# Two-block f32 forward pass on one core: expert panels in a ring of four groups of three, rows of 48 KB

## The chip, the core and the metric

One core of one Trainium2 chip runs the whole program. TensorE (PE) multiplies, VectorE (DVE) and ScalarE (ACT) work on what it leaves in PSUM, SyncE (SP) issues nearly all transfers from device memory (HBM) to the on-chip memory (SBUF, 128 partitions), and 16 DMA engines carry them. The metric is the device time of one execution in microseconds (us); the median of several executions stands for a kernel. The PE clock has two levels, 1.2 and 2.4 GHz; a granted clock of 1.00 in a stretch means the upper one throughout.

## The reference

Two blocks in sequence on 256 tokens of width 1024, all in f32. The first is a mixer (sliding-window attention, block attention, gated delta rule) and a gated feed-forward. The second puts 16 meta tokens in front (T = 272), runs a convolution branch and a bidirectional state-space branch, merges them, and ends with a mixture of experts. The end of the second block is what the change touches:

```python
branch_ssm  = y @ w_ssm_out                      # "ssm_out": 8 panels
branch_conf = ... @ w_conf_out                   # "conf_out": 4 panels
h = h + (gate_a * branch_conf + gate_b * branch_ssm) @ w_out     # "w_out_2": 4 panels
hn = rms_norm_2(h, w_norm_ffn)
aff = softmax(hn @ w_router)                     # 16 experts
top_aff, top_idx = top_k(aff.T, 34)              # each expert picks 34 of 272 tokens
for e in range(16):
    xg = hn[top_idx[e]]                          # 34 x 1024
    y[e] = (silu(xg @ w_gate[e]) * (xg @ w_up[e])) @ w_down[e]
h = h + scatter of top_aff[e] * y[e]
out = rms_norm_2(h[16:], w_norm_final)
```

Each expert has three matrices of 1024 x 2048 or 2048 x 1024 f32, 25.17 MB together; the 16 experts are 402.7 MB. Each weight is used once.

## The kernel before

All matrices are packed on the way in as panels, one contiguous row per partition. A panel of the dense stages is 128 x 2048 f32 (1.05 MB, rows of 8 KB). They go through two slots (`dense`, `slot_loaded`, `panel_done`, helper `panel` of SP's program, L370): SP issues the next panel into a slot when PE has finished the slot's last one. PE needs 32 matmuls, 7.37 us, for a panel of the second block.

An expert is twelve panels q = 0 to 11 of 128 x 4096 f32 (2.10 MB): q = 0 to 7 hold gate and up (even q is gate, odd q is up, one pair for each p = 0 to 3), q = 8 to 11 hold down. SBUF has a ring of `RING` = 12 slots, one for each q. The tensor `in_experts` is laid out as [16, 6, 128, 8192]: two neighbouring panels share a row of 32 KB. SP's program fills the ring with one transfer for two slots (`both[i]`, L474) where the slots are neighbours in SBUF, and slots 10 and 11 one by one (L477, L483). It waits until PE has released both (`ring_done[q]`). So an expert comes in five transfers of 4.19 MB with rows of 32 KB and two of 2.10 MB with rows of 16 KB.

Expert 0 is brought in during the stages before, slot by slot (`expert_panel`, L425; slot 11 at L403, near 120 us of the trace): each slot of the ring lies over buffers of an earlier stage and can be filled when they are dead. Slots 2 to 5 go behind the last four `ssm_out` panels, 10 behind the second `conf_out` panel, 0, 1 and 7 within and behind the `w_out_2` panels, then 6, 8 and 9. "Routing" is the short stage between the last `w_out_2` panel (near 873 us) and expert 0 (893.57 us): the logits, the softmax, the top-k and the first gather, with the turning of the tokens (`turn_tokens_of`) behind the logits.

Expert 1 replaces expert 0 in slots 0 to 3 by column parts, as soon as PE has read those columns (L461, `first_parts`). From slot 4 of expert 1 on, the loop at L462 to L486 runs. For the last expert, slots 6 and 7 come in two halves, 8 and 9 apart, 10 in two parts and 11 in three.

PE takes an expert in this order (`expert` for the first and last, `middle_expert` in a loop for the others): p = 0 reads slots 0 and 1 together; p = 1 reads slots 2 and 3, then the gather of the next expert's tokens; p = 2 reads 4 and 5; p = 3 reads 6 and 7; then slots 8 and 9, the scatter of the expert before, and slots 10 and 11. Every pair of slots is 32 matmul records of 128x512, some 7 us. PE waits on `pair_loaded[p]` ahead of each pair.

Of the kernel before, what the change touches and what calls it, by code (L numbers as in the profile page):

```python
# [11 lines left out]

# [10 lines left out]
P = 128  # L23
S = 256
META = 16
T = META + S
D = 1024
DC = D // P
PW = 256
# [9 lines left out]
E = 16  # L39
# [7 lines left out]
def pair_arrivals(i, e):  # L47

    return 2 + e + ((4 if i == 0 else 3) if i < 2 and e else 0)
# [29 lines left out]
def _run(kind, first, last):  # L79
# [29 lines left out]
             "last2_loaded": ("small_loaded", 16), "last9_loaded": ("last9_loaded", 0), "last10_loaded": ("last10_loaded", 0), "last_up": ("last_up", 0), "last3_loaded": ("rows_loaded", 16), "lgT_copied": ("wT_copied", 1), "lgT_done": ("res_ready", 4), "lg_done": ("heads_done", 2),  # L109
# [16 lines left out]
def two_blocks(nc, a, out):  # L126

    with ExitStack() as ctx:
# [174 lines left out]
        top[0] = upper  # L303
        cut(4 * 4096)
        es, up_row = cut(512), cut(512)
        lg, pos_t, aff = cut(3, E), cut(3, E), cut(3, E + 1)
        lmx, rst = cut(3), cut(3)
        m8 = cut(8)
        ss = cut(3, 4)
        xg = cut(DC, CAP)  # L310
        sum_col = cut(32)
        assert top[0] <= ARENA - 4096
# [6 lines left out]
        top[0] = mark1 - 512 - 2 * DC * T + 4096  # L319
        otT = [cut(S) for _ in range(2)]  # L320
        assert top[0] <= mark1
        top[0] = mark1 + 8192
        h_tok = cut(2, D)
        xt = cut(2 * 512)
        ysb, last_y = xt[64:64 + CAP, :], xt[0:CAP, 0:512]
        ones_r = cut(T)
        ohg, ohs = cut(2, CAP), cut(2, CAP)
        assert top[0] <= upper - 8192
        top[0] = mark1 - 512 - 2 * DC * T + 4096
        left, pos = cut(T), cut(T)  # L330
        assert top[0] <= mark1
        top[0] = low + 8192
        h_row = cut(2, 512)
        hx = cut(EB, CAP)
        assert top[0] <= base_dense + 2 * 11 * PW + DC * T
        pair_loaded = [ev(f"pair{i}_loaded") for i in range(5)]
        slot10_loaded, slot11_loaded = ev("slot10_loaded"), ev("slot11_loaded")
# [28 lines left out]
        def _(sp):  # L366
# [36 lines left out]
            sp.dma_start(ring[11], a["experts"][0, 5][:, 4096:8192]).then_inc(slot11_loaded, 16)  # L403
# [18 lines left out]
            def expert_panel(e, q):  # L422

                arrived = slot10_loaded if q == 10 else pair_loaded[q // 2]
                sp.dma_start(ring[q], a["experts"][e, q // 2][:, q % 2 * 4096:q % 2 * 4096 + 4096]).then_inc(arrived, 16)  # L425
# [12 lines left out]
            for g in range(4):  # L438
                panel(PANELS["w_out_2"] + g)
                if g == 1:  # L440
                    sp.wait_ge(ev("merged_ready"), after["merged_ready"] + 4)
                    expert_panel(0, 0)
            expert_panel(0, 1)
            expert_panel(0, 7)
            for last in (n[0] - 2, n[0] - 1):
                sp.wait_ge(panel_done[last % 2], last // 2 + 1)
            expert_panel(0, 6)
            sp.wait_ge(ev("lgT_done"), after["lgT_done"] + 1)
            expert_panel(0, 8)
            sp.wait_ge(ev("hacc_turned"), after["hacc_turned"] + 2)  # L450
            expert_panel(0, 9)
            in_parts = lambda ap: ap.rearrange("p (x m) -> p x m", x=2)
            for i, edges in enumerate(((0, 512, 1024, 2048, 3072, 4096), (0, 1024, 2048, 3072, 4096))):
                for j, (lo, hi) in enumerate(zip(edges, edges[1:])):
                    if hi < 4096:
                        sp.wait_ge(ev("first_parts"), after["first_parts"] + 4 * i + j + 1)
                    else:
                        sp.wait_ge(ring_done[2 * i], 1)
                        sp.wait_ge(ring_done[2 * i + 1], 1)
                    part = slice(lo, hi)  # L460
                    sp.dma_start(in_parts(both[i])[:, :, part], in_parts(a["experts"][1, i])[:, :, part]).then_inc(pair_loaded[i], 16)  # L461
            for e in range(1, E):  # L462
                for i in range(2 if e == 1 else 0, 5):
                    sp.wait_ge(ring_done[2 * i], e)
                    sp.wait_ge(ring_done[2 * i + 1], e)
                    if i == 4 and e + 1 == E:
                        sp.dma_start(ring[8], a["experts"][e, 4][:, 0:4096]).then_inc(pair_loaded[4], 16)
                        sp.dma_start(ring[9], a["experts"][e, 4][:, 4096:8192]).then_inc(ev("last9_loaded"), 16)
                    elif i == 3 and e + 1 == E:
                        for j, arrived in enumerate((pair_loaded[3], ev("last_up"))):  # L470
                            part = slice(2048 * j, 2048 * j + 2048)
                            sp.dma_start(in_parts(both[3])[:, :, part], in_parts(a["experts"][e, 3])[:, :, part]).then_inc(arrived, 16)
                    else:
                        sp.dma_start(both[i], a["experts"][e, i]).then_inc(pair_loaded[i], 16)  # L474
                sp.wait_ge(ring_done[10], e)
                if e + 1 < E:
                    sp.dma_start(ring[10], a["experts"][e, 5][:, 0:4096]).then_inc(slot10_loaded, 16)  # L477
                else:
                    for lo, arrived in ((0, slot10_loaded), (2048, ev("last10_loaded"))):
                        sp.dma_start(ring[10][:, lo:lo + 2048], a["experts"][e, 5][:, lo:lo + 2048]).then_inc(arrived, 16)  # L480
                sp.wait_ge(ring_done[11], e)
                if e + 1 < E:
                    sp.dma_start(ring[11], a["experts"][e, 5][:, 4096:8192]).then_inc(slot11_loaded, 16)  # L483
                else:
                    for lo, hi, arrived in ((0, 2, slot11_loaded), (2, 3, ev("last2_loaded")), (3, 4, ev("last3_loaded"))):
                        sp.dma_start(ring[11][:, 1024 * lo:1024 * hi],  # L486
                                     a["experts"][e, 5][:, 4096 + 1024 * lo:4096 + 1024 * hi]).then_inc(arrived, 16)
# [89 lines left out]
        def _(pe):  # L577
# [557 lines left out]
            pe.wait_ge(pair_loaded[1], 32)  # L1135
            for _ in range(6):
                mm(psum[:, 1, :], ident, ring[2][:, 0:512], start=True, stop=True)
# [1437 lines left out]
```

## Time and profile before

| | us |
|---|---|
| median of 3 runs | 1791.39 |
| lowest, highest | 1789.21, 1795.11 |
| the profiled execution, its own time | 1790.56 |
| its span in the trace | 1788.9 |
| start of the first expert's first matmul | 893.57 |
| start of the last expert's last 16 matmuls (slot 11) | 1775.52 |

The profile page gives busy time by engine (PE 1707.4 us, 95% of the span) and slices of the span. A busy share in a slice is an average. For the second half of this span two rows of the page have to be read side by side, that of PE and that of the DMA engines. PE counts as busy while its matmuls overlap, so a full PE row doesn't say that PE is what the end waits for; the waits do.

### The profile page before, as it was taken

The page shows a single profiled execution, that of the slowest core. Times are in us where ns is not written, and L with a number is a line of the kernel's source. Part 1 is how long each engine was busy: PE and PEld are TensorE (multiplying, and loading weights), DVE is VectorE, ACT ScalarE, POOL GpSimd, SP SyncE. Part 2 cuts the span into 40 slices and gives each one's busy share as a digit, 9 for nine tenths or more (in the row PEclk, how much of TensorE's full clock was granted, in tenths as well). Part 3 has the DMA queues.
Part 4 walks back from the last instruction along what each step waited for, and adds up shares of the span by engine and source line. Part 5 has one row for each costly group of instructions (what it writes and reads, how often), then busy time and mean ns, then how long its engine had stood idle before and what let it go on. Part 6 is the DMA issues. An engine that isn't in the chain of part 4 may idle for free.

```text
span 1788.9 us, 20978 instructions
## 1 busy us (share of the span) xinstructions
PE 1707.4 (95%) x8492; PEld 979.0 (55%) x8492; DVE 644.5 (36%) x1293; ACT 408.8 (23%) x783; POOL 32.3 (2%) x58
## 2 busy tenths in 40 slices
PE   9999999999999999999999999998988889998998
PEld 8778888887888888888723222322222222222222
DVE  3574466612759999941311101111010101111001
ACT  1143122201363544530111111111111111111112
POOL 4000000000000000100000000000000000000000
PEclk9999999999999999999999999989999999999989
DMA  5340244443453434376799999999999999999998
GB/s 187 118 189 13 83 158 148 163 148 115 167 191 118 167 129 169 108 284 250 311 388 432 430 428 435 428 432 432 431 430 431 430 430 434 430 432 428 435 431 332
DMA packets 36390, 523.08 MB, mean 292 GB/s; under 512 B 3880, under 2 KB 4072, under 8 KB 7784
## 3 DMA queue, kind: packets, MB, share of 16 engines
q1 hardware_dynamic: 35104, 511.75, 69.6%
q10 hardware_dynamic: 1224, 10.50, 1.6%
q8 instruction: 40, 0.66, 0.2%
q14 instruction: 22, 0.18, 0.0%
HBM read 521.12 MB, written 1.12 MB: 292 GB/s over the span
## 4 chain that ended last, share of the span: by engine, by line
PE 68%; DMA 27%; DVE 2%; SPq 1%; ACT 1%; issue 1%; DVEq 0%; another core or an unknown queue 0%; ACTq 0%
DMA arena<-in_experts 27%; PE psum L946 17%; PE psum L1301 12%; PE psum L597 12%; PE psum L1196 4%; PE psum L919 4%; PE psum L1030 3%; PE psum L1250 2%; PE psum L1011 1%; PE psum L660 1%; PE psum L681 1%; PE psum L899 1%; PE psum L1333 1%; PE psum L1220 1%; DMA arena<-in_panels 1%; SPq L480 1%
## 5 line engine op out<-in xcount | busy, mean ns | idle before, releaser
L1301 PE MATMUL psum<-arena 128*34 128x512 f32 x1792 | 412.2, 613 | 42.6 <-DMA arena<-in_experts 42.5
L2479 DVE SCALAR_TENSOR_TENSOR arena<-arena,psum 34x512 f32<-34x512 f32 x64 | 44.0, 687 | 759.5 <-ACT arena L1763 759.5
L946 PE MATMUL psum<-arena 128*128 128x272 f32 x1312 | 305.6, 392 | 0.0
L1301 PEld LDWEIGHTS psum<-arena 128*34 128x34 f32 x1792 | 106.5, 114 | 323.6 <-issue 279.1
L946 PEld LDWEIGHTS psum<-arena 128*128 128x128 f32 x1312 | 247.5, 189 | 53.2 <-issue 0.7
L1196 PE MATMUL psum<-arena 128*34 128x512 f32 x896 | 215.8, 637 | 9.8 <-DMA arena<-in_experts 9.8
L597 PE MATMUL psum<-arena 128*128 128x256 f32 x992 | 215.4, 378 | 0.0
L597 PEld LDWEIGHTS psum<-arena 128*128 128x128 f32 x992 | 187.2, 189 | 27.6 <-issue 1.2
L1196 PEld LDWEIGHTS psum<-arena 128*34 128x34 f32 x896 | 57.4, 118 | 157.9 <-issue 157.7
L1763 ACT ACTIVATE arena<-psum 34x512 f32<-34x512 f32 x64 | 37.9, 593 | 442.7 <-PE psum L1301 389.7
L2178 DVE SCALAR_TENSOR_TENSOR arena<-arena 128x272 f32<-128x272 f32 x240 | 111.0, 524 | 3.7
L919 PE MATMUL psum<-arena 128*128 128x256 f32 x352 | 76.4, 378 | 0.0
L919 PEld LDWEIGHTS psum<-arena 128*128 128x128 f32 x352 | 66.5, 189 | 9.7
L2166 DVE SCALAR_TENSOR_TENSOR arena<-arena 128x272 f32<-128x272 f32 x144 | 62.1, 498 | 6.6 <-ACT arena L1573 4.0
L1030 PE MATMUL psum<-arena 128*128 128x272 f32 x256 | 59.8, 392 | 0.1
L1250 PE MATMUL psum<-arena 128*34 128x512 f32 x256 | 56.4, 593 | 0.5 <-DVE arena L2460 0.5
L1783 ACT ACTIVATE arena<-psum 34x512 f32<-34x512 f32 x30 | 17.8, 592 | 169.1 <-PE psum L1196 161.8
L1333 PE MATMUL psum<-arena 34*128 34x512 f32 x112 | 55.0, 632 | 0.0
L1030 PEld LDWEIGHTS psum<-arena 128*128 128x128 f32 x256 | 48.3, 189 | 11.0 <-DMA arena<-in_panels 0.5
L2482 DVE SCALAR_TENSOR_TENSOR arena<-arena 34x512 f32<-34x512 f32 x64 | 44.0, 687 | 4.8
L1558 ACT ACTIVATE arena<-psum 128x544 f32<-128x544 f32 x34 | 21.2, 623 | 105.1 <-PE psum L946 103.8
L2098 DVE SCALAR_TENSOR_TENSOR arena<-arena 128x256 f32<-128x256 f32 x88 | 36.8, 482 | 4.5 <-issue 4.5
(449 smaller groups left out, 1368.9 us busy)
## 6 DMA issues: line engine op xcount, KB each, us to landing
arena<-in_experts SPq DMA_DIRECT2D x71, 4096.0 KB, 50.5
arena<-in_panels SPq DMA_DIRECT2D x91, 1024.0 KB, 4.8
arena<-in_experts SPq DMA_DIRECT2D x44, 2048.0 KB, 44.9
arena<-in_down_panels SPq DMA_DIRECT2D x8, 1408.0 KB, 6.0
arena<-in_experts SPq DMA_DIRECT2D x10, 1024.0 KB, 11.1
arena<-scr ACTq DMA_DIRECT2D x4, 2176.0 KB, 8.9
arena<-in_experts SPq DMA_DIRECT2D x4, 512.0 KB, 17.2
out<-arena SPq DMA_DIRECT2D x4, 256.0 KB, 2.1
```

Source lines behind the costliest of these rows:

```text
L597: ins = mm(pair[k][:, b, 0:width], slot8[k][:, c, b * P:(b + 1) * P], rhs(c), start=c == 0, stop=c == DC - 1)
L919: ins = mm(down_at(i)[:, b, :], slot11[k][:, c, b * P:(b + 1) * P], hid[:, 11 * j + c, :], start=j == 0 and i < 2 and c == 0, stop=j == 1 ...
L946: ins = mm(pair[k][:, b, 0:T], slot8[k][:, c, b * P:(b + 1) * P], src[:, c, :], start=c == 0, stop=c == DC - 1)
L1030: ins = mm(into[:, b, 0:T], slot8[k][:, c, b * P:(b + 1) * P], zT[:, 8 * j + c, :], start=j == 0 and c == 0, stop=j == 1 and c == DC - 1)
L1196: ins = mm(psum[64 * half:64 * half + CAP, 2, :], hx[:, f, :], r_dn[q][:, c, half * 512:(half + 1) * 512], start=f == 0, stop=f == EB - 1)
L1250: ins = mm(psum[lo:lo + CAP, p % 2, :], xg[:, c, :], r_up[2 * p + x][:, c, :], start=c == 0, stop=c == DC - 1)
L1301: ins = mm(psum[lo:lo + CAP, p % 2, :], xg[:, c, :], r_up[2 * p + x][:, c, :], start=c == 0, stop=c == DC - 1)
L1333: mm(psum[:, 4 + 2 * tb + half, :], otT[1 - par][64:64 + CAP, tb * P:(tb + 1) * P], ysb[:, half * 512:(half + 1) * 512], start=False, stop ...
L2166: ins = STT(gq[g % 2][:, b, :], xraw[g % 2][:, b, tap:tap + T], pcol("ssm_w", blk + 24 * tap), gq[g % 2][:, b, :], MUL, ADD)
L2178: STT(cc[:, c, :], cpad[:, c, tap:tap + T], pcol("conf_w", tap * DC + c), cc[:, c, :], MUL, ADD)
L2479: STT(es[gate_at, :], es[gate_at, :], 1.0, psum[gate_at, p % 2, :], ADD, MUL)
L2482: STT(h_row[turned_at, p % 2, :], es[gate_at, :], 0.5, up_row[gate_at, :], MUL, MUL).then_inc(ev("h_ready"), 1)
```

## The change

`in_experts` is laid out as [16, 4, 128, 12288]: three neighbouring panels share a row of 48 KB. The ring still has 12 slots, now in four groups of three (0 to 2, 3 to 5, 6 to 8, 9 to 11). Each group is contiguous in SBUF. The small buffers that lay between the slots move behind them. One transfer of 6.29 MB fills a group when PE has released all three of its slots. The exceptions are written out:

- Expert 0 still comes slot by slot. Slots 8, 7, 6 and 5 go behind the last four `ssm_out` panels, 4 behind the first `conf_out` panel, 3 behind the second, 2 where 0 was, then 1, 0, 9, and 10 with 11 in one. Nothing is loaded near 120 us.
- Expert 1: slots 0 and 1 in the same five parts; 2 and 3 in four parts, each part now two transfers; 4 and 5 in one.
- Expert 14 (last but one): its group 9 to 11 comes as 9 alone, then 10 with 11.
- Expert 15: 0 with 1, 2, 3, 4 with 5; from 6 on as before.

PE's arithmetic and its order are the same. Its waits ahead of the pairs become waits on groups: p = 0 on group 0, p = 1 and p = 2 on group 1, p = 3 and slot 8 on group 2, slot 9 on group 3. Three experts (13 to 15) are written out instead of one, and the loop runs six times instead of seven.

```diff
-        slots = [upper + 4096 * k for k in range(-2, 4)] + [mark1, mark1 + 4096, low, low + 4096, mark1 - 512 - 2 * DC * T, ARENA - 4096]
+        slots = [mark1 + 4096 * k for k in range(9)] + [low + 4096 * k for k in range(3)]
         ring = [arena[:, at:at + 4096] for at in slots]
-        both = [arena[:, slots[2 * i]:slots[2 * i] + 8192] for i in range(5)]
+        three = [arena[:, slots[3 * g]:slots[3 * g] + 3 * 4096] for g in range(4)]
...
-            sp.dma_start(ring[11], a["experts"][0, 5][:, 4096:8192]).then_inc(slot11_loaded, 16)
...
                 if i >= 4:
-                    expert_panel(0, i - 2)
+                    expert_panel(0, 12 - i)
             for g in range(4):
                 panel(PANELS["conf_out"] + g)
+                if g == 0:
+                    expert_panel(0, 4)
                 if g == 1:
-                    sp.wait_ge(ev("gates_tanh"), after["gates_tanh"] + 2)
-                    expert_panel(0, 10)
+                    sp.wait_ge(ev("conf_ready"), after["conf_ready"] + 1)
+                    expert_panel(0, 3)
...
-            expert_panel(0, 9)
+            sp.dma_start(three[3][:, 4096:], a["experts"][0, 3][:, 4096:]).then_inc(group_loaded[3], 16)
...
             for e in range(1, E):
-                for i in range(2 if e == 1 else 0, 5):
-                    sp.wait_ge(ring_done[2 * i], e)
-                    sp.wait_ge(ring_done[2 * i + 1], e)
...
+                for g in range(2 if e == 1 else 0, 4 if e + 2 < E else 3):
+                    for q in range(3 * g, 3 * g + 3):
+                        sp.wait_ge(ring_done[q], e)
+                    sp.dma_start(three[g], a["experts"][e, g]).then_inc(group_loaded[g], 16)
+            sp.wait_ge(ring_done[9], E - 2)
+            expert_panel(E - 2, 9)
+            for q in (10, 11):
+                sp.wait_ge(ring_done[q], E - 2)
+            sp.dma_start(three[3][:, 4096:], a["experts"][E - 2, 3][:, 4096:]).then_inc(ev("late_loaded"), 16)
...
                 for p in range(4):
-                    pe.wait_ge(pair_loaded[p], i * 32 + 16 * pair_arrivals(p, s + 1))
+                    pe.wait_ge(group_loaded[(0, 1, 1, 2)[p]], i * 32 + 16 * arrivals((0, 1, 1, 2)[p], s + 1))
```

The order of SP's transfers at three places. `in_panels` 128x2048 is a dense panel; `in_experts` 128x4096, 128x8192 and 128x12288 are one, two and three slots of the ring; the name behind "waits" is the semaphore (an event may share its semaphore's name with an older one: `bd_ready` is conf_ready, `o_copied` is gates_tanh).

SP from the last `ssm_out` panel's companion on, before:

```order
L425 DMA arena<-in_experts 128x4096
L370 DMA arena<-in_panels 128x2048 [waits panel_done1]
L370 DMA arena<-in_panels 128x2048 [waits panel_done0]
L425 DMA arena<-in_experts 128x4096 [waits o_copied]
L370 DMA arena<-in_panels 128x2048 [waits panel_done1]
```

and now:

```order
L426 DMA arena<-in_experts 128x4096
L372 DMA arena<-in_panels 128x2048 [waits panel_done1]
L426 DMA arena<-in_experts 128x4096
L372 DMA arena<-in_panels 128x2048 [waits panel_done0]
L426 DMA arena<-in_experts 128x4096 [waits bd_ready]
L372 DMA arena<-in_panels 128x2048 [waits panel_done1]
```

A slot of the ring (slot 4) now stands between the first and the second `conf_out` panel.

SP at the passage from expert 1's parts to the ring, from slots 4 and 5 of expert 1 on, before:

```order
L474 DMA arena<-in_experts 128x8192 [waits ring5_done,ring4_done]
L474 DMA arena<-in_experts 128x8192 [waits ring7_done,ring6_done]
L474 DMA arena<-in_experts 128x8192 [waits ring9_done,ring8_done]
L477 DMA arena<-in_experts 128x4096 [waits ring10_done]
L483 DMA arena<-in_experts 128x4096 [waits ring11_done]
L474 DMA arena<-in_experts 128x8192 [waits ring1_done,ring0_done]
```

and now:

```order
L475 DMA arena<-in_experts 128x8192 [waits ring5_done,ring4_done]
L482 DMA arena<-in_experts 128x12288 [waits ring8_done,ring7_done,ring6_done]
L482 DMA arena<-in_experts 128x12288 [waits ring11_done,ring10_done,ring9_done]
L482 DMA arena<-in_experts 128x12288 [waits ring2_done,ring1_done,ring0_done]
L482 DMA arena<-in_experts 128x12288 [waits ring5_done,ring4_done,ring3_done]
```

The transfer behind slots 4 and 5 now waits for slot 8 as well as for 6 and 7.

SP at the end, from expert 14's slots 6 and 7 on, before (the first two rows end expert 14's pairs):

```order
L474 DMA arena<-in_experts 128x8192 [waits ring7_done,ring6_done]
L474 DMA arena<-in_experts 128x8192 [waits ring9_done,ring8_done]
L477 DMA arena<-in_experts 128x4096 [waits ring10_done]
L483 DMA arena<-in_experts 128x4096 [waits ring11_done]
L474 DMA arena<-in_experts 128x8192 [waits ring1_done,ring0_done]
L474 DMA arena<-in_experts 128x8192 [waits ring3_done,ring2_done]
L474 DMA arena<-in_experts 128x8192 [waits ring5_done,ring4_done]
L472 DMA arena<-in_experts 128x2x2048 [waits ring7_done,ring6_done]
```

and now:

```order
L482 DMA arena<-in_experts 128x12288 [waits ring5_done,ring4_done,ring3_done]
L482 DMA arena<-in_experts 128x12288 [waits ring8_done,ring7_done,ring6_done]
L426 DMA arena<-in_experts 128x4096 [waits ring9_done]
L487 DMA arena<-in_experts 128x8192 [waits ring11_done,ring10_done]
L490 DMA arena<-in_experts 128x8192 [waits ring1_done,ring0_done]
L426 DMA arena<-in_experts 128x4096 [waits ring2_done]
L426 DMA arena<-in_experts 128x4096 [waits ring3_done]
L496 DMA arena<-in_experts 128x8192 [waits ring5_done,ring4_done]
L501 DMA arena<-in_experts 128x2x2048 [waits ring7_done,ring6_done]
```

Expert 14's slots 3 to 8 arrive in two transfers of three where they came in pairs and singles; what follows them is of the old sizes.

## Rows read from the trace of the kernel before

**Rows 1.** The page: span, and busy share of the DMA engines in 40 slices

```profile
span 1788.9 us, 20978 instructions
DMA  5340244443453434376799999999999999999998
```

**Rows 2.** Windows: us; busy us of each engine; PE clock, DMA share, GB/s

```profile
777.00:812.00 35.00, 34.91 (x152) 28.43 (x151) 8.73 (x5) 13.20 (x14) 0.00 (x0) 1.00 0.97 384
890.00:895.00 5.00, 4.46 (x31) 2.34 (x29) 1.97 (x6) 0.59 (x1) 0.00 (x0) 1.00 0.04 16
905.00:915.00 10.00, 10.00 (x48) 2.69 (x46) 1.38 (x2) 2.37 (x4) 0.00 (x0) 1.00 1.02 408
895.00:927.80 32.80, 32.80 (x166) 9.64 (x164) 6.75 (x13) 6.71 (x12) 0.00 (x0) 1.00 0.99 382
1174.00:1641.00 467.00, 424.08 (x1904) 130.16 (x1904) 54.17 (x104) 66.29 (x120) 0.00 (x0) 0.95 1.00 431
1755.00:1775.00 20.00, 19.80 (x103) 6.01 (x98) 2.75 (x4) 4.45 (x7) 0.00 (x0) 1.00 1.01 422
```

**Rows 3.** Timeline of PE, 1425 to 1500 us: start, duration, instructions, [idle before]

```profile
1437.22 7.08 PE L1301 MATMUL psum<-arena 128*34 128x512 f32 x32 [1.24 <-DMA arena<-in_experts]
...
1446.76 8.77 PE L1301 MATMUL psum<-arena 128*34 128x512 f32 x32 [2.06 <-DMA arena<-in_experts]
...
1495.58 4.92 PE L1301 MATMUL psum<-arena 128*34 128x512 f32 x22 [1.24 <-DMA arena<-in_experts]
```

**Rows 4.** DMA: SP's queue (packets, MB, share); issues by size, median to landing

```profile
q1 hardware_dynamic: 35104, 511.75, 69.6%
...
arena<-in_experts SPq DMA_DIRECT2D x71, 4096.0 KB, 50.5
...
arena<-in_experts SPq DMA_DIRECT2D x44, 2048.0 KB, 44.9
```

**Rows 5.** SP's timeline near 806 us, the chain there, and PE's timeline

```profile
806.42 8.05 SPq L370 DMA_DIRECT2D arena<-in_panels  x2
814.52 0.43 SPq L425 DMA_DIRECT2D arena<-in_experts  x1
...
799.06 7.38 DMA arena<-in_panels
...
813.95 29.63 PE L946 MATMUL psum<-arena 128*128 128x272 f32 x128
```

**Rows 6.** Timelines of SP and PE from routing into expert 1

```profile
858.70 23.94 SPq L425 DMA_DIRECT2D arena<-in_experts  x5
...
916.70 8.10 SPq L474 DMA_DIRECT2D arena<-in_experts  x2
...
925.06 7.06 PE L1220 MATMUL psum<-arena 128*34 128x512 f32 x32
...
947.68 7.08 PE L1301 MATMUL psum<-arena 128*34 128x512 f32 x32
```

**Rows 7.** PE: one undisturbed expert, then the end; SP's line L486 (slot 11)

```profile
1103.54 7.08 PE L1301 MATMUL psum<-arena 128*34 128x512 f32 x32
...
1145.87 4.47 PE L1301 MATMUL psum<-arena 128*34 128x512 f32 x20
...
1699.65 8.70 PE L1301 MATMUL psum<-arena 128*34 128x512 f32 x32 [1.80 <-DMA arena<-in_experts]
...
1721.37 9.76 PE L1196 MATMUL psum<-arena 128*34 128x512 f32 x32
1730.97 7.05 PE L1250 MATMUL psum<-arena 128*34 128x512 f32 x32
...
1775.52 3.63 PE L1220 MATMUL psum<-arena 128*34 128x512 f32 x16 [0.41 <-DMA arena<-in_experts]
...
L486 SPq DMA_DIRECT2D arena<-in_experts x3: 2135/2399/5725, 1740.4 to 1748.6; - x3
DMA to landing us min/median/max: 29.4/30.6/35.1
```

More of the change, by code:

```diff
@@ L44, with arrivals @@
 ARENA = 57048
-def pair_arrivals(i, e):
-    return 2 + e + ((4 if i == 0 else 3) if i < 2 and e else 0)
+def arrivals(g, e):
+    return (3, 3, 3, 2)[g] + e + ((4, 8, 0, 0)[g] if e else 0)
 SQ = {"x": 0, "qk": 4, "o": 5, "mix": 6, "h": 11, "ffn": 15, "h1": 20, "conf": 24}
@@ new lines, in two_blocks @@
+        h_tok = small(2, D)
+        xt = small(2 * 512)
+        ysb, last_y = xt[64:64 + CAP, :], xt[0:CAP, 0:512]
+        ones_r = small(T)
+        ohg, ohs = small(2, CAP), small(2, CAP)
+        es, up_row = small(512), small(512)
+        lg, pos_t, aff = small(3, E), small(3, E), small(3, E + 1)
+        lmx, rst = small(3), small(3)
+        m8 = small(8)
+        ss = small(3, 4)
+        xg = small(DC, CAP)
+        sum_col = small(32)
+        top[0] = low + 3 * 4096
+        left, pos = cut(T), cut(T)
@@ L320, in two_blocks @@
+        top[0] = low + 3 * 4096
+        h_row = cut(2, 512)
+        hx = cut(EB, CAP)
         otT = [cut(S) for _ in range(2)]
         assert top[0] <= mark1
[L322 to L337, printed above, removed]
+        group_loaded = [ev(f"group{g}_loaded") for g in range(4)]
         ring_done = [ev(f"ring{k}_done") for k in range(RING)]
@@ L450, in _ @@
             sp.wait_ge(ev("hacc_turned"), after["hacc_turned"] + 2)
-            expert_panel(0, 9)
[L452 to L461, printed above, removed]
@@ L462, in _ @@
-            for e in range(1, E):
-                for i in range(2 if e == 1 else 0, 5):
-                    sp.wait_ge(ring_done[2 * i], e)
-                    sp.wait_ge(ring_done[2 * i + 1], e)
[L466 to L487, printed above, removed]
@@ new lines, in _ @@
+            sp.dma_start(three[3][:, 4096:], a["experts"][0, 3][:, 4096:]).then_inc(group_loaded[3], 16)
+            pairs = lambda ap: ap.rearrange("p (x m) -> p x m", x=2)
+            edges = (0, 512, 1024, 2048, 3072, 4096)
+            for j, (lo, hi) in enumerate(zip(edges, edges[1:])):
+                if hi < 4096:
+                    sp.wait_ge(ev("first_parts"), after["first_parts"] + j + 1)
+                else:
+                    sp.wait_ge(ring_done[0], 1)
+                    sp.wait_ge(ring_done[1], 1)
+                sp.dma_start(pairs(three[0][:, 0:8192])[:, :, lo:hi],
+                             pairs(a["experts"][1, 0][:, 0:8192])[:, :, lo:hi]).then_inc(group_loaded[0], 16)
@@ new lines, in _ @@
+            for j in range(4):
+                if j < 3:
+                    sp.wait_ge(ev("first_parts"), after["first_parts"] + 5 + j)
+                else:
+                    sp.wait_ge(ring_done[2], 1)
+                    sp.wait_ge(ring_done[3], 1)
+                for q in (2, 3):
+                    expert_panel(1, q, group_loaded[1], 1024 * j, 1024 * j + 1024)
+            for q in (4, 5):
+                sp.wait_ge(ring_done[q], 1)
+            sp.dma_start(three[1][:, 4096:], a["experts"][1, 1][:, 4096:]).then_inc(group_loaded[1], 16)
@@ new lines, in _ @@
+            sp.dma_start(three[3][:, 4096:], a["experts"][E - 2, 3][:, 4096:]).then_inc(ev("late_loaded"), 16)
+            for q in (0, 1):
+                sp.wait_ge(ring_done[q], E - 1)
+            sp.dma_start(three[0][:, 0:8192], a["experts"][E - 1, 0][:, 0:8192]).then_inc(group_loaded[0], 16)
+            for q in (2, 3):
+                sp.wait_ge(ring_done[q], E - 1)
+                expert_panel(E - 1, q, ev("last1_loaded"))
+            for q in (4, 5):
+                sp.wait_ge(ring_done[q], E - 1)
@@ new lines, in _ @@
+            sp.dma_start(three[1][:, 4096:], a["experts"][E - 1, 1][:, 4096:]).then_inc(group_loaded[1], 16)
+            sp.wait_ge(ring_done[6], E - 1)
+            sp.wait_ge(ring_done[7], E - 1)
+            for j, arrived in enumerate((group_loaded[2], ev("last_up"))):
+                part = slice(2048 * j, 2048 * j + 2048)
+                sp.dma_start(pairs(three[2][:, 0:8192])[:, :, part],
+                             pairs(a["experts"][E - 1, 2][:, 0:8192])[:, :, part]).then_inc(arrived, 16)
@@ L1335, in middle_expert @@
                 pe.wait_ge(ev("hx_copied"), i * 4 + (2 * s + 4))
-                pe.wait_ge(slot10_loaded, i * 32 + 16 * (s + 2))
                 down_panel(10)
-                pe.wait_ge(slot11_loaded, i * 32 + 16 * (s + 2))
                 down_panel(11)
             expert(0)
-            with pe.Fori(0, (E - 2) // 2) as i:
+            with pe.Fori(0, (E - 4) // 2) as i:
                 for s in range(2):
                     middle_expert(i, s)
-            expert(E - 1)
+            for e in range(E - 3, E):
+                expert(e)
             scatter(E - 1)
```

73 lines of the change are left out of this document (41 added, 32 removed).

## The prediction

> **What bounds the kernel now.** I read the slices first. From about half the span on, the DMA engines are full to the end [rows 1]. That is the expert stage. The window from 1174 to 1641 us gives the load there: DMA share 1.00 at 431 GB/s, while PE is busy 424 of 467 us [rows 2]. PE's timeline says who waits: pairs of slots begin behind idle time that a transfer of in_experts ended, and the first pair of one expert begins 58.36 us after that of the one before (1437.22, 1495.58) [rows 3]. An expert is 25.17 MB, so 58.36 us is 431.2 GB/s. Undisturbed, PE needs less: one expert, from its second pair (1103.54) to the next one's first (1145.87) took 42.33 us [rows 7], and with the first pair and what goes with it about 51. So the end is set by a sum: when the DMA engines become full for good, the bytes left over their rate, and what PE still has to do once the last bytes are there. The change can move all three.
>
> **The larger rows.** Does the rate depend on the row? First, what counts as a packet. Each transfer of in_experts, in_panels and their like has 128 rows, or 256 where a part covers two slots (11 transfers). SP issues 234 transfers, 71 and 44 of them the large and the single ones of the ring [rows 4]. That makes 234 x 128 + 11 x 128 = 31,360 rows, and 16 completions for each transfer make 3,744 more: 35,104, which is the queue's count of packets exactly [rows 4]. So a row of 32 KB is one packet, and an engine handles 8 + 1 packets for a transfer of 128 rows. An expert costs it 7 x 9 = 63.
>
> The price of a packet comes from stretches that are full but cut finer. 1755 to 1775 us carries the last four slots in seven transfers: 63 packets where the ring has 21 for the same bytes, at 422 GB/s against 431 [rows 2]. 8.39 MB take 19.88 us against 19.45: 0.43 us for 42 packets, 10 ns each. 905 to 915 us carries parts with rows of 4 KB at 408 [rows 2]: 4.08 MB in 66 packets against 10, 0.54 us more, 9.6 ns. I take 10 ns.
>
> The change has 53 transfers of three slots, 333 MB or 13.25 experts. They cost 53 x 9 = 477 packets where the ring before has 13.25 x 63 = 835. The gain is 358 x 10 ns = **-3.6 us** (the ring at 433 GB/s). Its ends are 0, if a row of 48 KB is cut or something else holds the rate, and 13.6 ns a packet (what solving the ring and the last four slots with slightly other roundings gives), -4.9.
>
> The Trainium skill (DMA: Bandwidth & Descriptors, Bandwidth) puts the fabric's ceiling at 435.2 GB/s. By that, an expert's excess over the ceiling would be 0.54 us over 63 packets, 8.6 ns, and the gain -3.1 instead of -3.6.
>
> **The gap at group 2 of expert 1.** Before, the transfer of slots 6 and 7 is issued near 924.5, at the end of the two L474 issues that begin at 916.70 [rows 6]. From 895 to 927.8 the engines move 382 GB/s x 32.8 us = 12.5 MB [rows 2], which is slots 0 to 5 of expert 1 (12.58). So that transfer is there 3 us ahead of need. Now it also waits for slot 8. PE reads 8 and 9 in the 7.06 us from 925.06 [rows 6], so slot 8 is released at 928.6; the first bytes follow some 1.3 us behind the issue (an estimate, with ends of 0.3 and 2.0: at the panels below, bytes and what PE sees of them lie 1.8 us apart). The engines stand from 927.9 to about 930: **+2.1 us** (1.0 to 2.8). Every byte behind is moved by that, since the engines don't stand again: the next group is released near 940.3, while group 2 lasts to 944.5; group 0 of expert 2 is released when slots 2 and 3 are read, 954.6 (947.68 + 6.9) [rows 6], while group 3 lasts to 959; the lead then grows by 7 us with each expert.
>
> The idle time ahead of that, 890 to 895 at 16 GB/s [rows 2], is filled: slots 10 and 11 (4.19 MB in place of 2.10) are issued at the end of the five, 882.6 [rows 6], and last until 894. That costs nothing, since expert 1's first part is issued at 894.67 and PE needs slot 10 only near 933. It also gives nothing: the slot that moved there was free before, at 120 us. Slot 0, issued near 873 instead of 845, lands by 880 for a use at 893.57.
>
> **The conf_out panels.** From 777 to 812 us panels and slots share the engines at 384 GB/s [rows 2]. A panel is issued when its slot is released and is needed 7.37 us later. The one issued at 799.06 took 7.38, and the first conf_out panel (806.42) was begun at 813.95, 0.1 us late [rows 5]. By 806.42 four slots and five panels were issued, 13.6 MB, 13.4 of them in that window; so the engines were through at about 812.2, 1.8 us ahead of 813.95. Nothing is late again. Now slot 4 stands behind the panel of 806.42. It lasts to 812.2 + 5.2 = 817.4; the second panel (814.1) to 820.1, and seen 1.8 us behind, 821.9, for a need at 821.3. Slot 3 (in place of slot 10 at 814.52 [rows 5]) ends at 825.2, the third panel at 827.9, seen at 829.7 for a need at 829.3. **+0.9 us** on PE's path (0 if the engines move 431 there, 1.6 at the low end). PE's path leads through routing to the first parts, so the full stretch starts that much later.
>
> The wait of slot 3 for conf_ready costs nothing: PE waits for the same event before 813.95. PE's own waits on groups 0 to 3 for expert 0 are on slots landed 10 us or more ahead. The finer parts of slots 2 and 3 have the same rows as before. The unrolled experts have the same matmuls; I cost them at nothing.
>
> **The last two experts.** This is the term one overlooks. Before, PE ends level with the transfers: its last 16 matmuls begin at 1775.52 after 0.41 us of waiting and end at 1779.15; the last piece, issued at 1748.6, lands 29.4 later, at 1778.0 [rows 7]. Call that T. PE got there with no wait worth naming since 1699.65 [rows 7]. So anything that starts PE's last run later against T shows.
>
> Now the run starts earlier in the program but later against T. Expert 14's p = 1 waits for group 1. Behind its landing come group 2 (14.5 us), 9 to 11 (14.6) and expert 15 (58.8): it lands at T - 87.9. PE is idle some 6 us before it, since p = 0 needs group 0 alone, 14.5 us earlier. Such pairs mostly took 8.77 us where 7.08 is normal [rows 3], +1.7. Then 42.3 us to the next expert's first pair [rows 7], and from there to the end of slot 11 47.6 (1730.97 to 1779.15, less 0.6 of waits) [rows 7]; no piece lands later than PE wants it. Sum: T - 87.9 + 1.7 + 42.3 + 47.6 = T + 3.7, against T + 1.15 before: +2.5. A run of 91 us without a wait mostly holds one more slow stretch like 1721.37 (9.76 for 7.06) [rows 7]; I add 1.5 for it. **+4.0 us** (0.8 with neither, 5.8 with a long one).
>
> **Sum.** -3.6 + 2.1 + 0.9 + 4.0 = +3.4. The profiled execution took 1790.56, so 1794.0; it lies 0.83 below the median of 1791.39, so 1794.8 as a median.
>
> **Rivals.**
> A, the end is not late. If PE runs its last pairs at full clock and the gap at 928 is covered (the release comes while engines still work off expert 0's last slots), the terms are -3.6 + 1.0 + 0.5 + 0.8 = -1.3: 1790.1. For it: the bytes end and slot 8 is released within 1 us, and some pairs behind a wait ran at 7.08. Against: PE's wait before p = 1 is the longest of an expert. 0.18.
> B, the whole excess goes. The ring's 0.63 us per expert over 25.17 MB at 435.9 GB/s (the rate that 10 ns leaves) belongs to the pitch of 32 KB, not to packets, and 48 KB lifts all of it: 13.25 x 0.63 = -8.3, sum -1.3, 1790.1; with A's other terms, -6.0, 1785.4. For it: fine rows and the pitch can't be told apart in one trace. Against: the two finer stretches fit one price. 0.10. The Trainium skill (DMA: Bandwidth & Descriptors, Latency and other measured facts) has copies slowed by row pitches that are large powers of two, from 512 KB on; nothing here shows it at 32 KB.
> C, slower. Rows of 48 KB bring nothing: the ring keeps 431 GB/s, because a longer row is carried as two packets or a limit elsewhere holds. The losses stand: +7.0, 1798.4. The point from which this decides against the change is 3 ns a packet. For it: no row above 32 KB is in the trace. Against: 32 KB goes as one. 0.17.
> D, the panels are hit harder: if a longer run of both kinds loses twice what 777 to 812 us lost against the ring (337 GB/s), the two panels come 2.0 and 1.9 us late, +3.9 for 0.9, sum +6.4: 1797.8. 0.05.
> My forecast: 0.50.
>
> **Numbers.** A measurement of this kernel can tell about 0.3%, 5.4 us, from no change. The forecast's own spread, 1790.5 to 1798, is mostly inside; C and D are outside on the slow side, part of B on the fast. I add a little on the fast side for what isn't seen: faster 0.14, same 0.58, slower 0.28. The range runs from A and most of B to C and D with the medians' own 2 us: 1787 to 1800.
>
> **What would show it.** Right: the ring at 433 GB/s and an expert every 58.1 us; PE's share of windows alike; the engines standing near 929; in expert 15, PE with no wait on transfers and its last matmuls 3 to 6 us behind the last landing; SP's queue with fewer packets by exactly the count of rows and completions. Wrong: an expert still at 58.36 us (C), at 57.8 (B), last matmuls level with the last landing (A), conf_out panels begun more than 2 us late (D).

## The result and the profile after

| | before | changed | ratio, 95% interval |
|---|---|---|---|
| median, us (22 runs each) | 1791.24 | 1794.09 | 1.0018 [1.0011, 1.0024] |
| lowest, highest | 1788.32, 1795.11 | 1792.56, 1800.77 | |
| span in the trace | 1788.9 | 1791.8 | |

The changed kernel is 2.9 us slower, a small loss that 22 runs show clearly and that three would not. The forecast was 1794.8, 3.4 slower.

The page of the changed kernel, its span, its DMA slices, SP's queue, and the issues that answer to [rows 1, 4]:

```profile
span 1791.8 us, 20893 instructions
DMA  4330244433453444377799999999999999999997
...
q1 hardware_dynamic: 29408, 511.75, 69.4%
...
arena<-in_experts SPq DMA_DIRECT2D x53, 6144.0 KB, 40.5
```

The same bytes go in 29,408 packets where it was 35,104. The 5,696 that are gone are 356 for each of 16 engines. So a row of 48 KB is one packet too: an engine now handles 8 rows and one completion for three slots.

The windows that answer to [rows 2], and one more, of the end (us; busy time of each engine; PE clock, DMA share, GB/s), of the changed kernel:

```profile
777.00:812.00 35.00, 34.59 (x151) 28.15 (x150) 8.73 (x5) 12.36 (x13) 0.00 (x0) 1.00 0.99 396
...
890.00:895.00 5.00, 4.47 (x31) 2.39 (x29) 1.97 (x6) 0.59 (x1) 0.00 (x0) 1.00 0.99 421
...
925.00:935.00 10.00, 9.51 (x55) 3.32 (x56) 2.66 (x7) 1.41 (x3) 0.00 (x0) 1.00 0.94 374
1174.00:1641.00 467.00, 422.85 (x1917) 126.28 (x1915) 55.06 (x106) 67.67 (x122) 0.00 (x0) 0.94 1.00 433
```

```profile
1690.00:1745.00 55.00, 55.00 (x244) 16.69 (x241) 6.36 (x11) 8.69 (x16) 0.00 (x0) 0.95 0.99 426
```

Two windows of the kernel before that [rows 2] doesn't have:

```profile
925.00:935.00 10.00, 9.51 (x52) 3.03 (x52) 2.66 (x7) 1.01 (x3) 0.00 (x0) 1.00 0.99 424
1690.00:1745.00 55.00, 52.86 (x221) 16.16 (x223) 4.97 (x9) 6.56 (x13) 0.00 (x0) 0.91 1.01 432
```

The ring moves 433 GB/s, which was forecast; it was 431. The time before 895 us, empty in the kernel before, is full. In 925 to 935 us, where the kernel before has 424, the engines stand for a part: 374. In 1690 to 1745 us PE is busy without a pause; it was 52.86 of 55.00.

PE's timeline, which answers to [rows 3, 7]. First the second pair (p = 1) of two experts in the ring, then the last two experts, and the issue of the last two pieces:

```profile
1282.00 8.90 PE L1325 MATMUL psum<-arena 128*34 128x512 f32 x32 [6.49 <-DMA arena<-in_experts]
...
1340.06 8.77 PE L1325 MATMUL psum<-arena 128*34 128x512 f32 x32 [4.73 <-DMA arena<-in_experts]
```

```profile
1689.48 9.95 PE L1274 MATMUL psum<-arena 128*34 128x512 f32 x32 [5.30 <-DMA arena<-in_experts]
...
1771.51 10.50 PE L1241 MATMUL psum<-arena 128*34 128x512 f32 x48
...
L426 SPq DMA_DIRECT2D arena<-in_experts x2: 434/1262/2089, 1744.8 to 1747.0; - x2
DMA to landing us min/median/max: 31.3/31.7/32.1
```

PE now waits once per expert, for 4.7 to 6.7 us ahead of p = 1, where it mostly waited two to four times, for 1 to 2 us each. Two experts on, the same pair starts at 1398.26 and 1456.32; from 1165.72 to 1630.74 there are eight experts, 58.13 us each (it was 58.36). At the end there is no wait behind 1689.48: PE runs 92.5 us to 1782.01. The last piece is issued at 1747.0 and lands 31.3 later, at 1778.3; so PE ends 3.7 us behind it, where it was 1.15. The same distance was 3.7 to 5.3 us in all seven traces that leave the end as the change has it (the table in the section on why the prediction was right has them).

### The profile page after: what moved, and what is told of

It is laid out like the page before. It is cut to its first block, busy times and chain, and to the rows that moved or that the text cites. A ratio compares the mean times of both kernels' runs of the same rounds, so it can differ in the third digit from the quotient of the medians.

```text
span 1791.8 us, 20893 instructions
## 1 busy us (share of the span) xinstructions
PE 1701.8 (95%) x8490; PEld 971.4 (54%) x8490; DVE 644.8 (36%) x1293; ACT 409.9 (23%) x783; POOL 32.1 (2%) x58
## 3 DMA queue, kind: packets, MB, share of 16 engines
q1 hardware_dynamic: 29408, 511.75, 69.4%
## 4 chain that ended last, share of the span: by engine, by line
PE 70%; DMA 26%; DVE 2%; ACT 1%; issue 0%; DVEq 0%; ACTq 0%; SPq 0%
DMA arena<-in_experts 25%; PE psum L968 17%; PE psum L1325 12%; PE psum L619 12%; PE psum L1274 5%; PE psum L941 4%; PE psum L1052 3%; PE psum L1241 2%; PE psum L1218 2%; DMA arena<-in_panels 1%; PE psum L1033 1%; PE psum L682 1%; PE psum L703 1%; PE psum L921 1%; PE psum L1339 1%
## 5 line engine op out<-in xcount | busy, mean ns | idle before, releaser
L1325 PE MATMUL psum<-arena 128*34 128x512 f32 x1536 | 354.7, 615 | 49.2 <-DMA arena<-in_experts 49.2
L1218 PE MATMUL psum<-arena 128*34 128x512 f32 x768 | 182.9, 631 | 0.0
L1274 PE MATMUL psum<-arena 128*34 128x512 f32 x512 | 117.3, 611 | 11.0 <-DMA arena<-in_experts 10.4
L1241 PE MATMUL psum<-arena 128*34 128x512 f32 x256 | 58.1, 605 | 0.9 <-ACT arena L1799 0.5
L1357 PE MATMUL psum<-arena 34*128 34x512 f32 x96 | 45.9, 618 | 0.0
```

The costliest lines, as they stand in the source:

```text
L1218: ins = mm(psum[64 * half:64 * half + CAP, 2, :], hx[:, f, :], r_dn[q][:, c, half * 512:(half + 1) * 512], start=f == 0, stop=f == EB - 1)
L1241: ins = mm(psum[64 * half:64 * half + CAP, 2, :], hx[:, f, :], r_dn[q][:, c, half * 512:(half + 1) * 512], start=f == 0, stop=f == EB - 1)
L1274: ins = mm(psum[lo:lo + CAP, p % 2, :], xg[:, c, :], r_up[2 * p + x][:, c, :], start=c == 0, stop=c == DC - 1)
L1325: ins = mm(psum[lo:lo + CAP, p % 2, :], xg[:, c, :], r_up[2 * p + x][:, c, :], start=c == 0, stop=c == DC - 1)
L1357: mm(psum[:, 4 + 2 * tb + half, :], otT[1 - par][64:64 + CAP, tb * P:(tb + 1) * P], ysb[:, half * 512:(half + 1) * 512], start=False, stop ...
```

## Experiments

Eleven kernels were tried in twelve runs; one of them is the changed kernel itself. Ratios are to the kernel before, run beside them; its own medians there lay between 1791.05 and 1791.91.

| kernel | median, us | ratio, 95% interval |
|---|---|---|
| a1_gap | 1794.28 | 1.0015 [1.0007, 1.0024] |
| a2_tail | 1791.93 | 1.0003 [0.9992, 1.0013] |
| a3_panels | 1794.11 | 1.0017 [1.0008, 1.0025] |
| a4_all | 1789.30 | 0.9990 [0.9981, 0.9998] |
| a4_again | 1790.14 | 0.9999 [0.9990, 1.0008] |
| a5_singles | 1802.21 | 1.0055 [1.0035, 1.0075] |
| a6_two_one | 1798.42 | 1.0037 [1.0024, 1.0051] |
| b2_late11 | 1791.11 | 0.9991 [0.9982, 1.0001] |
| c1_gap_panels | 1792.72 | 1.0013 [1.0004, 1.0022] |
| c2_again (the changed kernel) | 1795.03 | 1.0020 [1.0011, 1.0030] |
| c3_tail_gap | 1790.54 | 1.0000 [0.9989, 1.0010] |
| c4_tail_panels | 1791.94 | 1.0003 [0.9993, 1.0013] |

### What a packet costs: a5_singles and a6_two_one

On the changed kernel, with PE's counts of arrivals made to fit (a6_two_one has the parts (0, 8192) and (8192, 12288)):

```diff
-                    sp.dma_start(three[g], a["experts"][e, g]).then_inc(group_loaded[g], 16)
+                    for lo, hi in ((0, 4096), (4096, 8192), (8192, 12288)):
+                        sp.dma_start(three[g][:, lo:hi], a["experts"][e, g][:, lo:hi]).then_inc(group_loaded[g], 16)
```

> The changed kernel with each of its 53 transfers of three slots issued as three transfers of one slot, at the same point and with PE's waits on the group as they are. Rows are 16 KB, their distance in device memory stays 48 KB. Price by packet (10 ns each): an engine has 27 packets for a group instead of 9, an expert takes 58.14 + 0.72 = 58.86 us, the median rises by 9.5 us to 1803.6. Rival (the distance of the rows made the gain): 58.14 us an expert, median 1794.

> The same with each transfer of three slots issued as one of two slots and one of one. Price by packet: 18 for 9, an expert takes 58.50 us, the median rises by 4.8 us to 1798.9. Rival: 58.14 us and 1794. A third case, a price by bytes of the row only where rows are below 32 KB, would put this one at half of a5_singles's rise or less.

PE's timeline of a5_singles, the second pair of the first and last of eight experts in a row, and the same of a6_two_one:

```profile
1169.54 9.40 PE L1329 MATMUL psum<-arena 128*34 128x512 f32 x32 [6.30 <-DMA arena<-in_experts]
...
1580.78 8.59 PE L1329 MATMUL psum<-arena 128*34 128x512 f32 x32 [5.33 <-DMA arena<-in_experts]
```

```profile
1170.90 9.60 PE L1329 MATMUL psum<-arena 128*34 128x512 f32 x32 [5.94 <-DMA arena<-in_experts]
...
1579.89 9.90 PE L1329 MATMUL psum<-arena 128*34 128x512 f32 x32 [5.34 <-DMA arena<-in_experts]
```

Seven experts lie between the rows of each pair. The four kernels stand on one line:

| kernel | packets of an engine for an expert | rows, their distance | us an expert | less 8.6 ns a packet |
|---|---|---|---|---|
| changed | 36 | 48 KB, 48 KB | 58.13 | 57.82 |
| before | 63 | mostly 32 KB, 32 KB | 58.36 | 57.82 |
| a6_two_one | 72 | 32 and 16 KB, 48 KB | 58.43 | 57.81 |
| a5_singles | 108 | 16 KB, 48 KB | 58.75 | 57.82 |

One price, 8.6 ns a packet, fits all four. The kernels with rows 48 KB apart lie on both sides of the kernel before in packets, and on its line. That settles the rival of the pitch (the distance from one row to the next), which would have put both splits at 58.13. The whole times agree as far as they can: 13.25 experts at 0.62 more are 8.2 us, and at 0.30 more 4.0. Against the kernel before, run beside them, the splits are 10.3 and 6.5 us slower, and the changed kernel is 2.9 slower: 7.4 and 3.6 for the splits alone. With four and seven runs these are good to 2 to 4 us.

What the line doesn't settle is whether the price belongs to the packet or to the transfer. In all four kernels an engine has nine packets for each transfer, so 77 ns a transfer would fit as well. One row of before speaks for the packet: in 905 to 915 us [rows 2] a transfer has 17 packets for an engine. By the packet that stretch would move 410 GB/s, by the transfer 422 (estimates from 66 packets or 3.9 transfers). It moved 408, and 413 in the trace of b2_late11. It is 10 us long, and no run was made for it.

What is left without packets is 57.82 us, 435.2 GB/s. The Trainium skill (DMA: Bandwidth & Descriptors, Bandwidth) gives that very figure as the ceiling of the fabric; this case agrees, since all four kernels come out at 57.81 or 57.82 us.

### The three losses: a1_gap, a2_tail, a3_panels and their sums

a1_gap, in SP's loop for expert 1 (its group 2 then has one arrival more):

```diff
+                if e == 1:
+                    sp.wait_ge(ring_done[6], 1)
+                    sp.wait_ge(ring_done[7], 1)
+                    sp.dma_start(three[2][:, 0:8192], a["experts"][1, 2][:, 0:8192]).then_inc(group_loaded[2], 16)
+                    sp.wait_ge(ring_done[8], 1)
+                    expert_panel(1, 8)
-                for g in range(2 if e == 1 else 0, 4 if e + 2 < E else 3):
+                for g in range(3 if e == 1 else 0, 4 if e + 2 < E else 3):
```

> The changed kernel with one edit: the first transfer of three, expert 1's slots 6 to 8, is issued as 6 with 7 and then 8 alone. My theory (the gap at group 2): 925 to 935 us goes from 374 GB/s back to about 424, the last landing comes 1.4 us earlier and the median falls by 1.4 us, to about 1792.7. Rival (the dip is only a shift of bytes between slices, or PE sets the end): the dip goes and the median stays within 0.4 us of the changed kernel's 1794.1.

a2_tail, for expert 14 (e = E - 2), with PE's waits on `last1_loaded` and `last8_loaded` used for both last experts:

```diff
-                for g in range(2 if e == 1 else 0, 4 if e + 2 < E else 3):
+                if e + 2 == E:
+                    break
+                for g in range(2 if e == 1 else 0, 4):
...
+            sp.dma_start(three[0][:, 0:8192], a["experts"][e, 0][:, 0:8192]).then_inc(group_loaded[0], 16)
+            for q in (2, 3):
+                sp.wait_ge(ring_done[q], e)
+                expert_panel(e, q, ev("last1_loaded"))
...
+            sp.dma_start(three[1][:, 4096:], a["experts"][e, 1][:, 4096:]).then_inc(group_loaded[1], 16)
...
+            sp.dma_start(three[2][:, 0:8192], a["experts"][e, 2][:, 0:8192]).then_inc(group_loaded[2], 16)
+            sp.wait_ge(ring_done[8], e)
+            expert_panel(e, 8, ev("last8_loaded"))
```

> The changed kernel with one edit: expert 14 comes as 0 with 1, 2, 3, 4 with 5, 6 with 7, 8 (and 9, 10 with 11 as in the change), PE waiting for each of them. Theory (PE ends late against the last landing): the wait of 5.3 us ahead of expert 14's second pair splits up or goes, PE's last matmuls end 1.2 us behind the last landing where it was 3.8, and the median falls by 2.3 us to about 1791.8. Rival (the transfers alone set the end): the last matmuls stay where they are, median 1794.1 to 1794.5 for three more transfers.

a3_panels:

```diff
-                if g == 0:
+                if g == 2:
                     expert_panel(0, 4)
```

> The changed kernel with one edit: slot 4 of expert 0 goes behind the third conf_out panel instead of the first. Theory (the conf_out panels): the wait of 0.6 us ahead of the third conf_out panel goes, everything behind it comes 0.5 to 0.9 us earlier, median about 1793.4. Rival: the wait moves to the fourth panel, no change.

> The three edits of a1_gap, a2_tail and a3_panels together on the changed kernel. Theory (the terms add): -1.4 - 2.3 - 0.7 = -4.4, median about 1789.7, which is 1.5 us below the kernel before; an expert in the ring takes 58.14 us as in the changed kernel. Rival (they hide one another, PE or the transfers being the same limit): the largest alone, about 1791.8.

**The traces** show each edit do what it was made for. The window of the gap in a1_gap:

```profile
925.00:935.00 10.00, 9.51 (x58) 3.32 (x54) 2.66 (x7) 1.58 (x3) 0.00 (x0) 1.00 1.00 431
```

The dip is gone, and expert 14's group 1 lands 794.0 us behind expert 0's start (1689.19 to 895.17) where the changed kernel has 795.5 (1689.48 to 893.96): 1.5 us. Over all traces without splits, the last landing lies 882.3 to 883.3 us behind expert 0's start with the edit (five traces) and 884.1 to 884.7 without (five): 1.7 us between the means.

PE's timeline of a2_tail, expert 14's second pair and the last 16 matmuls:

```profile
1685.63 7.08 PE L1293 MATMUL psum<-arena 128*34 128x512 f32 x32
...
1777.63 3.63 PE L1260 MATMUL psum<-arena 128*34 128x512 f32 x16 [0.42 <-DMA arena<-in_experts]
```

The second pair has no wait ahead of it, and the last matmuls wait 0.42 us for a transfer, as in [rows 7]. PE ends 1.2 us behind the last landing. The end is the transfers' again.

PE's timeline at the conf_out panels, of the changed kernel and then of a3_panels:

```profile
813.35 14.92 PE L968 MATMUL psum<-arena 128*128 128x272 f32 x64
828.86 15.00 PE L968 MATMUL psum<-arena 128*128 128x272 f32 x64 [0.60 <-DMA arena<-in_panels]
```

```profile
812.65 29.79 PE L968 MATMUL psum<-arena 128*128 128x272 f32 x128
```

With slot 4 behind the first panel the third one is late; with slot 4 behind the third panel all four run through. This repeats: the wait was 0.60, 0.87, 1.25, 1.24, 0.67, 0.32 and 0.42 us in the seven traces with slot 4 early (the changed kernel, a1_gap, a2_tail, the two splits, c2_again, c3_tail_gap), and there was none at that place in any other. From the start of the last five `ssm_out` panels (775.83, 775.81) to expert 0's (893.96, 892.42) the two kernels above take 118.1 and 116.6 us. That pair shows the edit at its best. The changed kernel's trace also has a wait of 0.41 us ahead of the last `ssm_out` panel, at 805.88, and so has a4_all's, with 0.74 there. The seven traces with slot 4 early take 117.1 to 118.4 us (mean 117.9), the five with the edit 116.6 to 117.8 (mean 117.2): 0.7 us.

**The medians** were less obliging. a2_tail came as expected; a1_gap and a3_panels alone moved nothing, against -1.4 and -0.7. Yet a4_all was 2.6 us below a2_tail. Either the single ones were high by chance, or an earlier landing helps only once the tail is mended. The remaining combinations were to tell:

> The edits of a1_gap and a3_panels together, without that of a2_tail. Each alone left the median where it was (1794.3 and 1794.1), though the traces show the landings 1.5 us earlier against expert 0's start (a1_gap) and expert 0's start 1.5 us earlier (a3_panels). Theory (they add, and the two medians were 1 to 1.5 us high by chance): 3 us faster than the changed kernel in the same call, about 1791. Rival (without the edit of the tail an earlier landing is lost again, since PE's last 93 us hold a slow stretch more): within 1 us of the changed kernel.

> The changed kernel again, as the measure for the others of this call. Both theories: 1794.1, ratio 1.0018 to the kernel before.

> The edits of a2_tail and a1_gap. Theory (terms add): 1.5 us below a2_tail's 1791.9, about 1790.4. Rival (the gap's 1.5 us count only together with the panels): 1791.9.

> The edits of a2_tail and a3_panels. Theory (terms add): 1.1 to 1.5 us below a2_tail, about 1790.6. Rival: 1791.9.

With c1 to c4 all eight combinations of the three edits are measured, so each edit is seen four times, against four different neighbours. With the means of the two measurements of the changed kernel (1794.56) and of a4_all (1789.72), in us:

| edit | alone | with one | with the other | with both | mean |
|---|---|---|---|---|---|
| gap | -0.3 | -1.4 (on tail) | -1.4 (on panels) | -2.2 | -1.3 |
| panels | -0.4 | -1.6 (on gap) | 0.0 (on tail) | -0.8 | -0.7 |
| tail | -2.6 | -3.7 (on gap) | -2.2 (on panels) | -3.0 | -2.9 |

A median's own uncertainty here is about 1 to 1.5 us, so hardly a single cell can be told from its mean. The means themselves have 95% intervals of -2.1 to -0.5 (gap), -1.4 to 0.1 (panels) and -3.6 to -2.0 (tail), an estimate from drawing again from the runs' times. So the tail's and the gap's terms are shown by time; that of the panels is not clear of nothing by time alone.

Single forecasts fared unevenly. c3_tail_gap came at its theory (1790.4, measured 1790.5), c4_tail_panels at its rival (1791.9). c1_gap_panels lies 2.3 us below the changed kernel run beside it, where one theory had 3 and the other less than 1; that speaks for plain addition. The gap's edit is worth -1.4 on a2_tail and on a3_panels alike. That the terms hide one another isn't needed, but times this wide don't exclude it.

> a4_all once more, in a call of its own with the kernel before. If its 1789.3 was no chance: ratio 0.999 again, about 1789.4. Rival (the best of eight by luck): 1791, ratio 1.000.

The second measurement gave 0.9999 where the first gave 0.9990, which is nearer to the rival. The best version is as fast as the kernel before, perhaps a microsecond faster; that it beats it isn't shown.

### The time at 120 us: b2_late11

On the kernel before:

```diff
-            sp.dma_start(ring[11], a["experts"][0, 5][:, 4096:8192]).then_inc(slot11_loaded, 16)
...
             expert_panel(0, 9)
+            sp.dma_start(ring[11], a["experts"][0, 5][:, 4096:8192]).then_inc(slot11_loaded, 16)
```

> The kernel before with one edit: slot 11 of expert 0 is issued behind slot 9, at 882 us instead of 120 us. Theory (it fills time in which the engines stood): 890 to 895 us is full, and the end doesn't move, ratio 1.000 with the spread of the runs. Second question: the traces of before and after differ near 132 us, where PE's clock was at 0.88 for 14 us beside that transfer and at 1.00 without it, 1.1 us. If the transfer does that, this kernel is 1 us faster and its clock there is 1.00 in the trace; if it is chance, nothing moves.

The window near 132 us of the kernel before, then the windows of b2_late11:

```profile
128.00:142.00 14.00, 11.48 (x263) 10.65 (x263) 9.40 (x26) 1.93 (x5) 0.00 (x0) 0.88 0.32 135
```

```profile
128.00:142.00 14.00, 11.38 (x263) 10.64 (x264) 9.48 (x26) 1.93 (x5) 0.00 (x0) 0.88 0.01 3
890.00:895.00 5.00, 4.46 (x31) 2.26 (x29) 1.97 (x6) 0.59 (x1) 0.00 (x0) 1.00 0.82 349
```

The load fills most of the empty stretch before 895 us, and the ratio's interval, 0.9982 to 1.0001, leaves room for at most 0.2 us of loss: moving it costs nothing. PE's granted clock is at 0.88 near 132 us with no transfer beside it. It is so too in the traces of a5_singles and c4_tail_panels, which are the changed kernel at that place, and 1.00 in the other ten of the change. So the transfer isn't needed for the lower clock, and the 1.1 us by which the trace of the changed kernel was ahead there isn't owed to the change.

## Why the prediction was right

The direction stood, and all four terms were found at their places. Their sizes were off, and that 3.4 came so close to 2.9 is in part luck: the three losses are smaller by time than forecast, the sum of the measured terms is 1.8, and something that isn't explained makes up the rest.

| term | forecast | measured by time | by the traces |
|---|---|---|---|
| larger rows | -3.6 | | -3.1: 8.6 ns x 356 packets; four kernels on one line |
| gap at group 2 | +2.1 | +1.3 (mean of four) | 1.5 to 1.7 (last landing, with and without the edit) |
| conf_out panels | +0.9 | +0.7 (mean of four) | 0.7 (with and without the edit) |
| last two experts | +4.0 | +2.9 (mean of four) | 2.5 to 4.1, mean 3.4 (PE's end against the last landing, to before) |
| sum | +3.4 | +1.8 (with -3.1 for the rows) | the whole: +2.9 measured |

The losses stand as what their edits gave back. The gap's and the tail's edits cost 9 and 27 packets an engine, some 0.1 and 0.2 us, which would have to be added.

- **Rows.** Counting packets was the step that carried the argument. The price was read 1.4 ns too high, from two short windows whose rates are given to 1 GB/s. The sentence on the ceiling (-3.1 instead of -3.6) was the better number. The runs show the gain directly for eight experts in a row (58.36 to 58.13 us); for the other experts it is worked out.
- **Gap.** Place and cause were right; the engines stood for 1.2 to 1.7 us instead of 2.1. SP issued the transfer at 929.18 (forecast 928.6). The 1.3 us from there to the first bytes was an estimate, no run measures it, and which part of the 2.1 was too long stays open.
- **Panels.** The prediction had the second panel 0.6 us late and the third 0.4. The second was on time; the third was late, by 0.3 to 1.3 us. So the price came out of the right mechanism, mostly at the neighbouring panel. The sum behind it slips as well: it lets a slot last 5.2 us, but at the 384 GB/s that it reads a slot takes 5.5, and the same reckoning then gives about 1.7, its own upper end.
- **Last two experts.** Group 1 of expert 14 landed 88.8 us before the last piece (forecast 87.9), and PE needed 92.5 (forecast 93.1). So PE ended 3.7 us late in this trace, where the forecast with its slow stretch had 5.2 and without it 3.7. Here the pair at 1689.48 took 9.95 instead of 8.77, and nothing after it was slow. In the traces of a1_gap, a3_panels, c2_again and both splits the same run held one more slow stretch (15.59 to 15.65 us for four slots that take 13.96 else) and lasted 93.2 to 93.7 us, and PE ended 4.7 to 5.3 us late. So the separate 1.5 us was right in five traces of seven.
- **Rivals.** A (the end is not late) falls with 3.7 us and with a2_tail. B (pitch) falls with the line of four kernels. C (rows bring nothing) falls with 58.13. Its 3 ns a packet isn't where gain and loss cancel; against its own +7.0 that takes some 20 ns (7.0 us over 358 packets). D (panels at 337 GB/s) falls: from 806 to 829 us the engines moved 416 to 425 GB/s in the three traces where they were full (a6_two_one, c2_again, c3_tail_gap), and no panel was 2 us late.

What stays open can be placed by cutting each trace at common events:

| stretch, us | before, b2_late11 | the change, this edit absent | with this edit |
|---|---|---|---|
| last five `ssm_out` panels to expert 0's start (panels) | 116.8, 116.5 | 117.1 to 118.4, mean 117.9 (7) | 116.6 to 117.8, mean 117.2 (5) |
| expert 0's start to the last landing (gap; no splits) | 884.4, 884.2 | 884.1 to 884.7, mean 884.3 (5) | 882.3 to 883.3, mean 882.7 (5) |
| last landing to PE's end (tail) | 1.2, 1.2 | 3.7 to 5.3, mean 4.6 (7) | 1.2 (5) |

The number of traces stands in brackets. With the edit of the gap the second stretch should be 2.8 to 3.0 us shorter than before (3.1 for the rows, less 0.1 to 0.3 for the edits' packets); it is 1.6 shorter. The first stretch stays 0.5 us longer even with the edit of the panels. So some 1.3 us of the rows' gain don't show, between expert 0's start and the last landing. That is also why a4_all and a4_again, which mend three terms and keep the rows, are 1.5 us below the kernel before instead of 2.8, and it fits the 1.1 us that the sum of 1.8 lacks. In the ring itself the gain is whole: eight experts at 58.12 or 58.13 us in every trace of the change without splits. From 1690 to 1745 us the engines move 426 GB/s in the changed kernel and 432 in the kernel before, with a full queue in both, which is 0.8 us. A PE that is busy throughout is not the reason: in the trace of a4_again it pauses for 2.1 us in that window, and the rate is 426 too. The cause wasn't tried and stays open.

## What to carry to other kernels

When transfers bound a stage, count its packets (one for each contiguous row, and one for each engine and transfer): the price of one, times those saved, is what longer rows brought here. It was a sixth of a per cent, while the coarser pieces cost more at three edges outside the steady ring: where the ring starts, where other loads share the engines, and at the end.

The bound of the end isn't the bound of the stage. Before making arrivals coarser, reckon backwards from the last landing how long the consumer still runs after the last arrival that it had to wait for; the last two rounds may need the small pieces even if the others don't.

## What the runs showed of the hardware

- A packet costs a DMA engine 8.6 ns beside its bytes, the same for rows of 16, 32 and 48 KB, and a full queue moves 435.2 GB/s less that (58.13, 58.36, 58.43 and 58.75 us for an expert at 36, 63, 72 and 108 packets). With nine packets to every transfer, a price of 77 ns a transfer would fit these four too. The distance of the rows in device memory, 32 or 48 KB, made no difference.
- PE's first pair after a wait of 5 to 7 us took 8.4 to 10.1 us for the 7.08 of full clock; the granted clock was 0.79 in one of 8.90 us and 0.70 in one of 9.95 us (1282.00 and 1689.48 in the changed kernel). The time drifted from expert to expert: in a5_singles 9.40, 9.07, 8.68, then 10.05, 9.65, 9.32, 8.91, 8.59. Waits of 1 to 2 us were followed by either 7.08 or 8.5 to 8.8. So the length of a wait alone didn't tell what it cost PE, and one trace of a changed end can be off by some 1.5 us (PE ended 3.7 us behind the last landing in one trace of the changed kernel and 5.3 in another).
- In two traces of the same changed kernel expert 0 started at 893.96 and at 897.44 us after the span's start, and over all 14 traces at 892.4 to 897.8. Stretches should be compared from a common event, not from the start of the span.
